# Forgetting attention with the values held stationary, two heads on the column halves of the array, and output products by tile

## What is computed

```python
def fox_attention(q, k, v, log_f):
    c = cumsum(log_f)                       # per head
    for i in range(S // 128):               # blocks of 128 queries, keys up to the block's end
        s = q_block @ k[:end].T * scale + c[block][:, None] - c[None, :end]
        s = where(key <= query, s, -inf)
        p = softmax(s)
        out[block] = p @ v[:end]
# parallel_mixer: concatenate([fox_out, gla_out]) @ w_out   (512 + 512 inputs, 1024 outputs)
```

## Time and profile before

| | us |
|---|---|
| median of three runs | 1668.95 |
| the profiled execution, whole | 1670.93 |
| its span in the profile | 1669.1 |
| PE busy | 1470.0 |
| DVE busy | 479.6 |
| ACT busy | 339.9 |
| the stage of the change, from the first scores (1368.5) to the end of the output product (1410.85) | 42.3 |

### The profile page before, as it was taken

One profiled execution on the slowest core, in us unless ns is written; L12 is line 12 of the kernel. 1 busy time (PEld: TensorE's weight loads), 2 busy tenths in 40 slices (PEclk: granted clock), 3 DMA queues, 4 the chain that ended last, 5 costly groups with the idle time before them and its releaser, 6 DMA issues. The chain is left out here.

```text
span 1669.1 us, 17593 instructions
## 1 busy us (share of the span) xinstructions
PE 1470.0 (88%) x7708; PEld 825.9 (49%) x7708; DVE 479.6 (29%) x728; ACT 339.9 (20%) x515; POOL 118.9 (7%) x113
## 2 busy tenths in 40 slices
PE   4999979889888899799798878878888999999999
PEld 2755642242242243299532323323324767788897
DVE  1487440100100000156500001001004754345443
ACT  1122410000000000134200000000003645544442
POOL 0000010000000000010100000000003044330000
PEclk9999989999989999999899999999999999999999
DMA  9989969999999999996499999999999844244510
GB/s 375 410 347 413 396 223 429 416 428 427 416 430 427 412 428 427 410 397 239 145 417 422 428 427 421 429 426 423 428 425 353 292 174 150 103 148 169 189 51 26
DMA packets 93298, 563.06 MB, mean 337 GB/s; under 512 B 8048, under 2 KB 9448, under 8 KB 53670
## 3 DMA queue, kind: packets, MB, share of 16 engines
q1 hardware_dynamic: 89504, 551.77, 81.2%
q0 software_dynamic: 2384, 9.42, 1.6%
q10 hardware_dynamic: 1334, 0.75, 0.2%
HBM read 558.74 MB, written 3.17 MB: 337 GB/s over the span
## 5 line engine op out<-in xcount | busy, mean ns | idle before, releaser
L2231 PE MATMUL ps<-ring,scratch 128*32 128x512 f32 x2048 | 432.5, 608 | 60.0 <-DMA ring<-in_moe_w_up 27.5
L2231 PEld LDWEIGHTS ps<-ring,scratch 128*32 128x32 f32 x2048 | 127.9, 112 | 351.6 <-issue 344.2
L2210 PE MATMUL ps<-ring,scratch 128*32 128x512 f32 x1024 | 205.3, 603 | 28.7 <-DMA ring<-in_moe_w_down 28.7
L1946 PE MATMUL ps<-ring_parts,scratch_parts 128*128 128x512 f32 x656 | 186.9, 403 | 5.0 <-DVE xT_parts L1208 1.4
L1946 PE MATMUL ps<-scratch_parts,ring_parts 128*128 128x256 f32 x704 | 146.1, 283 | 0.0
L1946 PEld LDWEIGHTS ps<-ring_parts,scratch_parts 128*128 128x128 f32 x656 | 122.6, 189 | 33.2 <-DVE xT_parts L1208 1.6
L2210 PEld LDWEIGHTS ps<-ring,scratch 128*32 128x32 f32 x1024 | 50.3, 111 | 159.2 <-issue 107.8
L614 ACT ACTIVATE ring_parts<-ring 128x2048 fp32r<-128x2048 f32 x56 | 106.4, 1919 | 93.1 <-PE ps L1946 86.5
L463 DVE TENSOR_TENSOR ring_parts<-ring,ring_parts 128x2048 fp32r<-128x2048 f32 x46 | 105.6, 2297 | 54.9 <-ACT ring_parts L614 53.9
L1946 PEld LDWEIGHTS ps<-scratch_parts,ring_parts 128*128 128x128 f32 x704 | 114.8, 189 | 0.3
L1534 DVE TENSOR_TENSOR scratch<-ps,gate_bc 128x512 f32<-128x512 f32 x16 | 11.1, 692 | 253.2 <-PE ps L2210 253.2
(11 more groups left out here) (393 smaller groups left out, 1565.1 us busy)
## 6 DMA issues: line engine op xcount, KB each, us to landing
ring<-in_moe_w_gate SPq DMA_DIRECT2D x64, 2048.0 KB, 30.0
ring<-in_moe_w_up SPq DMA_DIRECT2D x64, 2048.0 KB, 18.7
ring<-in_moe_w_down SPq DMA_DIRECT2D x64, 2048.0 KB, 30.2
ring<-in_ada_w SPq DMA_DIRECT2D x24, 2048.0 KB, 13.9
ring<-in_mlp_w SPq DMA_DIRECT2D x16, 2048.0 KB, 8.8
ring<-in_sc_w_in SPq DMA_DIRECT2D x6, 2048.0 KB, 21.7
ring<-in_w_in SPq DMA_DIRECT2D x6, 2048.0 KB, 20.3
ring<-in_xattn_wkv SPq DMA_DIRECT2D x4, 2048.0 KB, 35.5
```

Of the source, the lines that this page charges most:

```text
L1946: last = mm(out, lhs[x], rhs[y], start=start and n == 0, stop=stop and n == 2)
L2210: last = mm(ps[32 * j:32 * j + 32, banks[half], :], src[:, k, CAP * j:CAP * (j + 1)], w[:, e, col:col + 512], start=(k == 0), stop=(k == K ...
L2231: last = mm(ps[32 * j:32 * j + 32, banks[half], :], src[:, k, CAP * j:CAP * (j + 1)], w[e][:, 0, col:col + 512], start=(k == 0), stop=(k = ...
```

## The change

On PE the two heads of a pair q (heads 2q and 2q+1) are handled together. The value product is turned round: the values of one head (128 keys x 64) are stationary and the transposed probabilities (128 keys x 128 queries) move. The even head's product lands on partitions 0 to 63 and the odd one's on 64 to 127 of bank FO[t], at the columns of their k-tile, so the result is already transposed (features on partitions). The eight row transposes at the end are gone.

Since the row sums would now lie along columns, the probabilities are divided ahead of their transposes: DVE waits for both exponentials of the pair, takes two reciprocals, and multiplies each head's probabilities by its own (16 new instructions of 128x128 or 128x256, 8 small reciprocals), in place of the two 128x512 multiplications. fp has four buffers instead of two.

The lists are reordered. PE, for pair q: scores of pair q+1, one or two w_out blocks of half 1, values of pair q-1, transposes of both heads of q. DVE: weights of q, logits and maxima of the two heads of q+1, copy of the even transposes. ACT: the two exponentials of q+1, copy of the odd transposes. The split of tile 0's result stands behind pair 4's copies on ACT and DVE (`fox_high(0)`, `fox_low(0)`), that of tile 1 at the end. The two roundings of w_out's half 0 stand behind pairs 5 and 6 on ACT. 14 of the 16 blocks of half 1 lie in the loop, 2 between the last transposes and the last values. The blocks of half 0 run by tile: both chunks for token tile 0, then both for tile 1; each half counts as used at the end of its tile 1. `fox_x[0]` moves from scratch to the rows buffer, since fp takes its place.

```diff
-        fp = at(5632, b=2, s=N)
+        fp = at(5632, b=4, s=N)
-        fox_x = (x_hi[:, 4:8], xT_r[:, 0:4])
+        fox_x = (rows_hi[:, 0:4], xT_r[:, 0:4])
-        OUT_BLOCKS_AT = (0, 1, 2, 3, 4, 6, 8, 9, 11, 12, 13, 14)
+        OUT_BLOCKS = ((0, 1), (2,), (3,), (4, 5), (6, 7), (8, 9), (10, 11), (12, 13))
# ACT
+            def fox_high(t):
+                act.wait_ge(sem("fx_pv"), FOX_PAIRS // 2 * (t + 1))
+                nc.scalar.activation(tile_cols(fox_x[0], t), pb(FO[t]).rearrange("p (k q) -> p k q", k=4), ACT.Copy)\
+                    .then_inc(sem("x_high"), 1)
+            fox_probs(0)
+            fox_probs(1)
+            for q in range(FOX_PAIRS):
+                mk = P * (2 * q // FOXH + 1)
+                for n in (2 * q + 2, 2 * q + 3):
+                    if n < 2 * FOX_PAIRS:
+                        fox_probs(n)
+                act.wait_ge(sem("fx_pT_ps"), 2 * q + 2)
+                if q:
+                    act.wait_ge(sem("fx_pv"), q)
                 nc.scalar.activation(fpT[:, 1, 0:mk], ps[:, FTB[1], 0:mk], ACT.Copy).then_inc(sem("fx_pT_act"), 1)
+                if q == FOX_PAIRS // 2:
+                    fox_high(0)
+                if q in (FOX_PAIRS // 2 + 1, FOX_PAIRS // 2 + 2):
+                    high(FIRST["w_out"] + q - FOX_PAIRS // 2 - 1, (0,))
+            fox_high(1)
# DVE
+            def fox_weights(q):
+                c = slice(112 + 2 * q, 114 + 2 * q)
+                dve.wait_ge(sem("fx_p"), 2 * q + 2)
+                link(nc.vector.reciprocal(sm[:, c], sm[:, 96 + 2 * q:98 + 2 * q]))
+                for n in (2 * q, 2 * q + 1):
+                    x = fp[:, fox_buffer(n), 0:P * (n // FOXH + 1)]
+                    nc.vector.tensor_scalar(x, x, sm[:, 112 + n:113 + n], None, ALU.mult).then_inc(sem("fx_weights"), 1)
+            fox_logits(0)
+            fox_logits(1)
+            for q in range(FOX_PAIRS):
+                mk = P * (2 * q // FOXH + 1)
+                fox_weights(q)
+                for n in (2 * q + 2, 2 * q + 3):
+                    if n < 2 * FOX_PAIRS:
+                        fox_logits(n)
+                dve.wait_ge(sem("fx_pT_ps"), 2 * q + 1)
+                if q:
+                    dve.wait_ge(sem("fx_pv"), q)
+                nc.vector.tensor_copy(fpT[:, 0, 0:mk], ps[:, FTB[0], 0:mk]).then_inc(sem("fx_pT_dve"), 1)
+                if q == FOX_PAIRS // 2:
+                    fox_low(0)
+            fox_low(1)
# PE
+            def fox_values(q):
...
+                for s in range(t + 1):
+                    for n in (2 * q, 2 * q + 1):
+                        hd, o = n % FOXH, 64 * (n % 2)
+                        last = mm(ps[o:o + 64, FO[t], P * (hd // 2):P * (hd // 2 + 1)], fv[:, s, HD * hd:HD * (hd + 1)],
+                                  fpT[:, n % 2, P * s:P * (s + 1)], start=(s == 0), stop=(s == t))
             fox_scores(0)
+            pe.wait_ge(sem("x_split"), 4 * SPLIT_INPUTS.index("w_out") + 2)
+            for q in range(FOX_PAIRS):
+                if q + 1 < FOX_PAIRS:
+                    fox_scores(q + 1)
+                else:
+                    pe.wait_ge(sem("fx_max"), NT * FOXH)
+                for b in OUT_BLOCKS[q]:
                     if b == 8:
-                        pe.wait_ge(sem("mix_rows"), 2)
+                        input_split("w_out", 2)
                     w_out_block(b // 8, b % 8)
+                if q:
+                    fox_values(q - 1)
+                fox_transposed(2 * q)
+                fox_transposed(2 * q + 1)
+            for b in (6, 7):
                 w_out_block(1, b)
+            fox_values(FOX_PAIRS - 1)
+            fox_block(0, 0)
+            fox_block(1, 0).then_inc(sem("tile_0_whole"), 1)
+            fox_block(0, 1).then_inc(sem("w_halves_used"), 2)
+            fox_block(1, 1).then_inc(sem("w_halves_used"), 2)
```

More of the change, by code:

```diff
@@ L327, in gates_stored, with fox_buffer, tile_cols @@
             eng.wait_ge(sem(GATE_OUT[g]), 2 * 16 * list(GATE_OUT.values()).count(GATE_OUT[g]))
+        def fox_buffer(n):
+            return 2 * (n // 2 % 2) + n % 2
+        def tile_cols(v, t):
+            return v[:, :, P * t:P * (t + 1)]
         def ada_chunk(g, c):
@@ L388, in build @@
         FT = ((4, 5), (6, 7))
-        FOX_AT = FOXH + 2
+        FOX_PAIRS = NT * FOXH // 2
         XQT = (4, 5, 6, 7)
@@ L920, in _, with fox_probs @@
             scaled_rows("w_fv", fv, FO)
[L922 to L926, removed]
-                nc.scalar.activation(fpT[:, 1, 0:mk], ps[:, FTB[1], 0:mk], ACT.Copy).then_inc(sem("fx_pT_act"), 1)
[L929 to L939, removed]
+            def fox_probs(n):
+                nk = P * (n // FOXH + 1)
+                x = fp[:, fox_buffer(n), 0:nk]
+                act.wait_ge(sem("fx_max"), n + 1)
+                nc.scalar.activation(x, x, ACT.Exp, bias=sm[:, 64 + n:65 + n],
+                                     accum_out=sm[:, 96 + n:97 + n]).then_inc(sem("fx_p"), 1)
+            def fox_high(t):
[12 more added lines that the diff above has]
+                    act.wait_ge(sem("fx_pv"), q)
+                nc.scalar.activation(fpT[:, 1, 0:mk], ps[:, FTB[1], 0:mk], ACT.Copy).then_inc(sem("fx_pT_act"), 1)
+                if q == FOX_PAIRS // 2:
[3 more added lines that the diff above has]
+            fox_high(1)
             high(FIRST["wq"])
@@ L982, in _ @@
             x_probs(4)
-            columns_high(16, (4, 5), x_hi)
+            columns_high(14, (4, 5), x_hi)
             x_probs(5)
@@ L1775, in _, with fox_logits @@
             columns_low("w_out", 0, WO[0], gla_x[1], gla_x[0])
[L1777 to L1787, removed]
+            def fox_logits(n):
                 t, hd, nk = n // FOXH, n % FOXH, P * (n // FOXH + 1)
-                x = fp[:, n % 2, 0:nk]
-                if n == FOX_AT:
-                    fox_rows(0)
+                x = fp[:, fox_buffer(n), 0:nk]
                 dve.wait_ge(sem("fx_s"), n + 1)
-                if n >= 2:
-                    dve.wait_ge(sem("fx_pT_ps"), n - 1)
+                if n >= 4:
+                    dve.wait_ge(sem("fx_pT_ps"), n - 3)
                 if n % FOXH == 0:
@@ L1799, in _, with fox_low @@
                 nc.vector.tensor_reduce(sm[:, 64 + n:65 + n], x, AX.X, ALU.max, negate=True).then_inc(sem("fx_max"), 1)
[L1800 to L1807, removed]
+            def fox_weights(q):
[5 more added lines that the diff above has]
+                    nc.vector.tensor_scalar(x, x, sm[:, 112 + n:113 + n], None, ALU.mult).then_inc(sem("fx_weights"), 1)
+            def fox_low(t):
+                dve.wait_ge(sem("x_high"), 4 * SPLIT_INPUTS.index("w_out") + 2 + t + 1)
+                nc.vector.tensor_tensor(tile_cols(fox_x[1], t), pb(FO[t]).rearrange("p (k q) -> p k q", k=4),
+                                        tile_cols(fox_x[0], t).bitcast(F32), ALU.subtract).then_inc(sem("x_split"), 1)
+            dve.wait_ge(sem("ccol"), 1)
+            fox_logits(0)
[13 more added lines that the diff above has]
+            fox_low(1)
             add_plain(2, "w_out", WO[0] + WO[1])
@@ L2480, in _, with fox_scores @@
             row_transposes(gr, WO[0], range(4))
[L2483 to L2489, removed]
+            def fox_scores(q):
+                for n in (2 * q, 2 * q + 1):
+                    t, hd = n // FOXH, n % FOXH
+                    if q:
+                        pe.wait_ge(sem("fx_max"), n - 1)
+                    s, nk = slice(64 * (hd % 2), 64 * (hd % 2) + 64), P * (t + 1)
+                    mm(ps[:, FS[n % 2], 0:nk], fT[s, 0, hd // 2, P * t:P * (t + 1)], fT[s, 1, hd // 2, 0:nk],
+                       start=True, stop=True).then_inc(sem("fx_s"), 1)
             def fox_transposed(n):
-                pe.wait_ge(sem("fx_p"), n + 1)
+                pe.wait_ge(sem("fx_weights"), n + 1)
                 if n >= 2:
@@ L2516, in _, with fox_block @@
             fox_scores(0)
[L2517 to L2522, removed]
+            pe.wait_ge(sem("x_split"), 4 * SPLIT_INPUTS.index("w_out") + 2)
[5 more added lines that the diff above has]
+                for b in OUT_BLOCKS[q]:
                     if b == 8:
-                        pe.wait_ge(sem("mix_rows"), 2)
+                        input_split("w_out", 2)
                     w_out_block(b // 8, b % 8)
[L2526 to L2537, removed]
-                w_out_block(1, b)
-            for j in range(2):
-                split_half(FIRST["w_out"] + j, 0, fox_x, WO[j], j == 1, (1, 0), ("w_out", 2) if j == 0 else None).then_inc(sem("w_halves_used"), 2)
+                if q:
+                    fox_values(q - 1)
+                fox_transposed(2 * q)
+                fox_transposed(2 * q + 1)
+            for b in (6, 7):
+                w_out_block(1, b)
+            fox_values(FOX_PAIRS - 1)
+            def fox_block(j, t):
+                if j == 0:
+                    input_split("w_out", 2 + t)
+                for kk in range(4):
```

(6 more changed lines are left out.)

19 lines of the change are left out of this document (9 added, 10 removed).

## The result

| | before | after |
|---|---|---|
| median, 13 runs each, us | 1669.27 | 1672.79 |
| ratio (95% interval) | | 1.0021 (1.0012 to 1.0029) |
| profiled execution, its span, us | 1670.93, 1669.1 | 1671.04, 1669.2 |

A forecast was written before the change was run, and what follows sets the result against it. PE was taken as the bound, 88% busy, about even with the DVE and ACT loop inside the stage. Stage -0.2 plus wq wait +0.8 gave +0.6: 1671.5 us profiled, 1669.6 for the median; range 1665.5 to 1674.

The forecast's parts named there:

- The loop: Round of division, logits, maxima, exponentials through DVE and ACT: 2.4 us at 128 keys, 3.2 at 256, about even with PE.
- The turned product: Value products on PE, per pair: 0.57 us for 128 keys and about 0.9 for 256, against 0.34 and 0.78.
- the sign of being wrong that the prediction names itself: Forecast wrong if the value product costs far from 0.6 and 0.9 us, or a 256-key round isn't near 3.3 us.
- the lower of my two bounds: Eight value-product records for 256 keys: between 0.58 us, if the second four overlap, and 0.74.
- The +1.4 us of PE work: Eight turned value products, shape change taken once per pair: 4 x 0.23 + 4 x 0.12; ends +0.2 and +2.
- Row transposes: Eight row transposes removed from PE's path at the stage's end: -0.87 us, if PE stays the bound there.
- The division of pair 7: DVE's multiplications by a column ahead of the last pair's transposes: 0.35 us each at 256 keys.
- The moved queue: w_out's roundings behind pairs 5 and 6, so POOL's two low parts run from about 1392.9 to 1402.2.
- The 0.2 us wait ahead of fox_block(1, 0): The block, reached at 1402.1, waits for POOL's low parts of w_out, which end at 1402.2.
- wq behind the stage: First wq product waits for POOL's low part, ending 1414.5 and wanted at 1413.7: +0.8 us.
- The first rival: Half-clock stretches after PE standstills, early and ahead of block 8, cost 1.75 us each; two give +4.1, 1673.1; chance 0.19.

The follow-up runs named there:

- e7: Changed kernel with each pair's four value products for 256 keys issued head by head, not key tile by key tile; 0.60 us against 0.59, no ratio.
- e2: Changed kernel with the low parts of w_out's half 0 made by DVE and not POOL; ratio to the kernel before 1.0007 (0.9998 to 1.0017).
- e1: Changed kernel with half 0 of w_out run chunk after chunk again; ratio to the kernel before 1.0004 (0.9995 to 1.0013).
- e4: Kernel before with only the 16 blocks of half 0 run by tile; ratio to the kernel before 1.0008 (0.9999 to 1.0016).
- e6: Changed kernel dividing by a two-operand multiplication with broadcast column; gated rows' transposes to span's end 309.57 us, against 304.48 in the changed kernel; no ratio.
- e8: Changed kernel, half 0 chunk after chunk, its low parts on DVE, gated rows' transposes and block 0 earlier, first rounds thinned; ratio to before 1.0005 (0.9996 to 1.0014).
- f3: Kernel before with one idle matmul (0.86 us) in PE's 1.15 us standstill ahead of the first block; ratio to the kernel before 0.9989 (0.9980 to 0.9999).

## Why the forecast came out as it did

The time, 1672.79, lies in the stated range, and I had the sign of the sum right (+0.6); the size was +3.5, and it ends a little beyond the 0.2% where I had put only 0.16 of the chance. The range, 8.5 us wide, held it; the forecast itself, 1669.6, missed by nearly the whole of the change. Point by point:

- **The loop.** The starts of the pairs' divisions, counted from the gated rows' transposes (1367.55 and 1364.72), were forecast at 4.3, 7.1, 9.7, 12.1, 15.2, 20.0, 23.3 and 26.9 us. Measured: 4.3, 7.3, 9.8, 12.2, 15.2, 19.8, 23.0 and 26.3. The hop by hop sum holds, half clock and the wait for `fox_low(0)` included (1.39 us of PE against 1.7).
- **The turned product.** Forecast 0.57 and 0.9 us, measured 0.37 and 0.59 to the next start, which is the sign of being wrong that the prediction names itself. Rows of after, tile 0 and tile 1:

```profile
1378.63 0.44 PE L2544 MATMUL ps<-scratch 128*64 128x128 f32 x4
1379.00 0.44 PE L2531 MATMUL ps<-cst,scratch 128*128 128x128 f32 x2
...
1386.23 0.66 PE L2544 MATMUL ps<-scratch 128*64 128x128 f32 x8
1386.82 0.66 PE L2531 MATMUL ps<-cst,scratch 128*128 128x128 f32 x4
```

  Two steps of the working failed. The 0.2 us for the change of shape doesn't stand beside the product: it falls on the blocks (two take 1.60, 0.80 each, and one alone 0.90, against the 0.76 I had used). And I said that the row of 0.37 shows no gain from the two halves. It has the gain in it: a single product took 0.36 in the same rows, as told under e7. For 256 keys the lower of my two bounds, 0.58, was the right one. The +1.4 us of PE work was mis-sized: with 0.34 and 0.78 before, it is 4 x 0.03 - 4 x 0.19 for the products, plus 12 x 0.04 and 2 x 0.14 for the 14 blocks in the loop, about nothing.
- **Row transposes.** From the last values' end to the first transpose of h: 14.6 us before, 11.0 after, as forecast.
- **The division of pair 7: the missed step.** I took 0.35 us for each multiplication from a row that ran with POOL idle and put POOL's low parts at 1392.9 to 1402.2 in the next paragraph, across pair 7's division, without asking whether the two engines get in each other's way. Cost: 2.9 us of DVE, 1.7 of PE's standing still, 1.8 of the stage (e2). Without it the stage is 1.43 us shorter than before (e2: 41.71 against 43.14), and not 0.2. So two misses of opposite sign stood in that term, and the stage came out at +0.37, near the forecast, by luck.
- **The moved queue.** POOL's low parts ran from 25.1 to 34.5 us behind the anchor; forecast 25.3 to 34.7. The 0.2 us wait ahead of fox_block(1, 0) did not come, since the last values were later than forecast.
- **wq behind the stage.** +0.8 forecast, +1.01 measured, by the mechanism named: e1 takes it away, e4 brings it into the kernel before.
- **The clock.** The first rival had the mechanism and the price (1.75 us a stretch; 1.55 measured) but not the place. It looked ahead of block 8, where 1.39 us of standing still left the clock full, and at the start, where after has one stretch of 3.4 us as before. The stretch came behind the wait that I had myself put at 0.8 us on top of 1.18. I summed that wait as time alone.

So two of the three losses were side effects that stood in my own timetable: a pair of engines at work at once, and a longer standstill of PE.

## What to carry to other kernels

When a step moves, write down what every other engine runs at its new time, and price the pair and not the instruction: 0.62 us became 3.54 beside POOL. Look for the counter that a reordered loop moves: the same 16 blocks in another order made the next stage's weights 2.8 us late against the end of the stage. A standstill of PE costs its own length and perhaps a half-clock stretch behind it, and a version that thins PE's load to let another engine through can lose more than it wins. And before a row is taken as a price, compare it with the rows beside it: the 0.37 us for two products stood beside 0.36 for one, and so held the overlap that I had missed.

## What the runs showed of the hardware that I had not expected

- A DVE multiplication with its operand in SBUF waits for a POOL instruction that is under way, to its end: 3.29 us for 0.35. With two SBUF operands it lost twice in a row: two multiplications took 8.09 us for 0.76 (e6).
- The half clock is not tied to one standstill. The same wait of 2.2 us was followed by it in after, e4 and e7, and not in e2 and e6; a stretch of 3.4 us there cost 1.54 to 1.61. Around PE's standstill of 4.20 us it lasted 6.8 us (e6), and behind the thinned rounds 10 us (e8); with an idle matmul in the old gap it came 14.5 us later (f3). Which execution gets it is left open, and with it how much of the timed 3.5 us it is.
- Float32 products of 128 columns on the two column halves run two at a time: eight records take 0.22 us more than four, 0.11 for each pair, and on the whole array a single record takes 0.11 (half of the 0.22 for 256 columns). The order of the halves in the program makes no difference (e7).
